# One block of the r, k and v groups' vectors on TensorE and three on VectorE, instead of two and two

## The reference

```python
def trunk(x, c, ...):
    cs = jax.nn.silu(c)                                   # one condition vector for prompt, one for sample
    for l in range(DEPTH):
        mod = (cs @ W['ada_w'][l] + W['ada_b'][l]).reshape(B, N_MOD, D)   # 6 vectors of 2048 each
        h = modulate(rmsnorm(x, W['norm_mix_g'][l]), mod[:, 0], mod[:, 1])
        ...
        r = (h + xx * mu[0]) @ p['wr']                    # 288 tokens x 2048 x 2048
        k = (h + xx * mu[2]) @ p['wk']
        v = xv @ p['wv']
```

## Time and profile before

| what | value |
|---|---|
| time, median of 3 runs | 3187.66 us (3185.27 to 3188.28) |
| profiled execution, its own time | 3181.33 us |
| its span | 3179.8 us |
| TensorE (PE) busy | 3099.7 us, 97% of the span |
| TensorE weight loads (PEld) busy | 2933.2 us, 92% |
| VectorE (DVE) busy | 2301.4 us, 72% |
| ScalarE (ACT) busy | 1405.9 us, 44% |
| stream loads | 1022 of 512 KB, 4.2 us from issue to landing (median) |

### The profile page before, as it was taken

The page is one execution under the profiler, slowest core; times in us unless marked ns, Lnnn a source line. Parts: engine busy times, 40 slices in busy tenths (PEclk is TensorE's granted clock), DMA queues, the critical chain, the costliest instruction groups (busy, mean ns, idle before and its releaser), DMA issues.

```text
span 3179.8 us, 80532 instructions
## 1 busy us (share of the span) xinstructions
PE 3099.7 (97%) x31192; PEld 2933.2 (92%) x31192; DVE 2301.4 (72%) x4445; ACT 1405.9 (44%) x2322; POOL 196.9 (6%) x371
## 2 busy tenths in 40 slices
PE   6999999998999999999999999999999999999998
PEld 3799988877999999999999989998999999999998
DVE  3676777776478978888788888778785566666655
ACT  2333336665355443343344744334455534343442
POOL 0000000110000000000000000101100000000000
PEclk8999999999999999999999999999999999999999
DMA  9887750003878887777777444644554455556443
GB/s 394 327 296 294 291 196 21 23 23 126 328 292 288 305 297 270 244 239 251 243 247 248 169 146 150 220 158 150 187 175 165 165 202 203 204 204 207 169 164 117
DMA packets 184093, 667.94 MB, mean 210 GB/s; under 512 B 22646, under 2 KB 22816, under 8 KB 183360
## 3 DMA queue, kind: packets, MB, share of 16 engines
q1 hardware_dynamic: 149184, 545.78, 47.3%
q0 software_dynamic: 34688, 119.07, 11.7%
HBM read 660.68 MB, written 4.09 MB: 209 GB/s over the span
## 4 chain that ended last, share of the span: by engine, by line
PE 91%; DMA 3%; DVE 3%; issue 1%; ACT 1%; SPq 0%; DVEq 0%; POOLq 0%; ACTq 0%
PE ps L2384 52%; PE ps L2367 8%; PE ps L2369 7%; PE ps L2368 7%; PE ps L2553 5%; DMA sb_raw<-stream 2%; PE ps L2318 1%; PE ps L2545 1%; DMA sb_late_w<-late 1%; PE ps L2883 1%; PE ps L2884 1%; PE ps L2885 1%; PE ps L2927 1%; PE ps L2926 1%; PE ps L2329 1%
## 5 line engine op out<-in xcount | busy, mean ns | idle before, releaser
L786 ACT ACTIVATE sb_whi<-sb_raw 128x1024 fp32r<-128x1024 f32 x778 | 811.0, 1057 | 1089.7 <-PE ps L2384 674.0
L1278 DVE TENSOR_TENSOR sb_wlo<-sb_raw,sb_whi 128x1024 fp32r<-128x1024 f32 x778 | 943.4, 1222 | 318.2 <-ACT sb_whi L786 315.5
L2384 PE MATMUL ps<-sb_ah,sb_whi 128*128 128x288 f32 (+1 forms) x2776 | 485.4, 297 | 1.2 <-DVE sb_wlo L1278 1.2
L2384 PE MATMUL ps<-sb_al,sb_whi 128*128 128x288 f32 (+1 forms) x2776 | 483.2, 296 | 0.0
L2384 PE MATMUL ps<-sb_ah,sb_wlo 128*128 128x288 f32 (+1 forms) x2776 | 481.1, 295 | 0.0
L2384 PEld LDWEIGHTS ps<-sb_ah,sb_whi 128*128 128x128 f32 x2776 | 408.6, 189 | 5.8 <-issue 3.1
L2384 PEld LDWEIGHTS ps<-sb_al,sb_whi 128*128 128x128 f32 x2776 | 408.0, 189 | 0.0
L2384 PEld LDWEIGHTS ps<-sb_ah,sb_wlo 128*128 128x128 f32 x2776 | 407.2, 188 | 0.0
L2367 PE MATMUL ps<-sb_ah,sb_whi 128*128 128x288 f32 (+1 forms) x952 | 286.5, 301 | 4.1 <-DVE sb_x L1531 3.2
L2369 PE MATMUL ps<-sb_al,sb_whi 128*128 128x288 f32 (+1 forms) x952 | 283.1, 297 | 0.0
L2368 PE MATMUL ps<-sb_ah,sb_wlo 128*128 128x288 f32 (+1 forms) x952 | 282.5, 297 | 0.0
(11 more groups left out here) (366 smaller groups left out, 4797.0 us busy)
## 6 DMA issues: line engine op xcount, KB each, us to landing
sb_raw<-stream SPq DMA_DIRECT2D x1022, 512.0 KB, 4.2
sb_strip<-strips POOLq DMA_DIRECT2D x124, 512.0 KB, 5.0
sb_late_w<-late POOLq DMA_DIRECT2D x96, 256.0 KB, 3.2
sb_gate_w<-late POOLq DMA_DIRECT2D x64, 256.0 KB, 3.6
sb_x<-xT SPq DMA_DIRECT2D x1, 2304.0 KB, 15.8
sb_x<-xT POOLq DMA_DIRECT2D x1, 2304.0 KB, 11.0
yT<-sb_x SPq DMA_DIRECT2D x4, 576.0 KB, 2.8
sb_lwa<-lw POOLq DMA_DIRECT2D x16, 130.0 KB, 2.5
```

The source lines that it names most:

```text
L786: nc.scalar.activation(whi[:, q % SPL, :], raw[:, n, :], ACT.Copy).then_inc(hi_ready, 1)
L1278: nc.vector.tensor_tensor(wlo[:, q % SPL, :], raw[:, n, :], whi[:, q % SPL, :], ALU.subtract).then_inc(lo_ready, 1)
L2384: ins = mm(PS[:, m, 0:s.wide], w[:, n % SPL, a:a + P], z[:, 2 * p + j, 0:s.wide], start=False, stop=False)
```

## The change

In the nine shared groups TensorE takes one block of vectors instead of two, and VectorE three instead of two. TensorE's block now fills two slots (`BURST_SLOTS`), buffers 0 and 1 of round A, and is done in 16 products of 2 x 128 columns. VectorE's three blocks fill six slots (`ROW_SLOTS`): buffers 2 and 3 of round A and 0 to 3 of round B. Row slot 0 and the copy to `arow` now stand behind the split of slot 2, row slot 1 behind that of slot 3, row slots 2 and 3 behind slot 4, row slot 4 behind slot 5 and row slot 5 behind slot 6. `half_finish` turns one block. The stream has as many bytes as before; SP's instructions are the same ones in the same order.

```diff
+ROW_SLOTS = 6
+BURST_SLOTS = 2 * BURST - ROW_SLOTS
+GROUP_ROWS = ROW_SLOTS // 2
+STAGE_BURSTS = 4 + 3
-SHARED_PLACES = ((), (0, 1), (2,), (3,), (), ())
+SHARED_PLACES = ((0,), (1,), (2, 3), (4,), (5,), ())
...
                 if shared(s, it):
-                    dve.wait_ge(ada_used, 2 * BURST * g + BURST)
+                    dve.wait_ge(ada_used, 2 * BURST * g + BURST_SLOTS)
...
-                if i == 2:
+                if i == 0:
                     row(s, it)
                 for j in SHARED_PLACES[i]:
                     one_row_strip(s, it, j)
...
-                dve.wait_ge(landed[j], it * s.span * 2 + 16 * ((s.n0 + RAW + j) // RAW + 1))
-                dve.wait_ge(ada_used, 2 * BURST * it + (2 * BURST * s.ada0 + BURST + j))
+                dve.wait_ge(landed[n % RAW], it * s.span * 2 + 16 * (n // RAW + 1))
+                dve.wait_ge(ada_used, 2 * BURST * it + (2 * BURST * s.ada0 + BURST_SLOTS + j))
                 for e in range(4):
                     a, z = e // 2, e % 2
...
-                        out=PS[:, 6 + z, :], in0=raw[:, j, ROW * a:ROW * a + ROW], scalar=1.0, in1=crows[z][:],
+                        out=PS[:, 6 + z, :], in0=raw[:, n % RAW, ROW * a:ROW * a + ROW], scalar=1.0, in1=crows[z][:],
...
                 pe.wait_ge(arow_ready, s.ada0 + it)
-                for p in range(BURST):
+                for p in range(BURST_SLOTS):
                     n = s.n0 + p
                     pe.wait_ge(landed[n % RAW], it * s.span * 2 + 16 * (n // RAW + 1))
-                    for z in range(4):
-                        ins = mm(PS[32 * z:32 * z + 2, 4, 0:256], cs[:, 4 * p + z, :], raw[:, n % RAW, 256 * z:256 * z + 256],
-                                 start=p == 0, stop=p == BURST - 1)
+                    for b in range(8):
+                        z = b % 4
+                        ins = mm(PS[32 * z:32 * z + 2, 4, 0:P], cs[:, 8 * p + b, :], raw[:, n % RAW, P * b:P * b + P],
+                                 start=p == 0 and b < 4, stop=p == BURST_SLOTS - 1 and b >= 4)
                     ins.then_inc(ada_used, 1)
...
-                for m in range(2):
+                for m in range(blocks):
                     ins = mm(PS[:, 5, 2 * m:2 * m + 2], arow[:, P * m:P * m + P], con[:, SEL + 4:SEL + 6],
                              start=True, stop=True)
...
                         if shared(s, it) and p == 6:
-                            half_finish(s.ada0 + it)
+                            half_finish(s.ada0 + it, 1)
```

More of the change, by code:

```diff
@@ L239 @@
 SHARED0 = BY["r"].ada0 * 4
-ROW_BLOCKS0 = SHARED0 + 10 * len(SHARED)
-SHARED_PLACES = ((), (0, 1), (2,), (3,), (), ())
+ROW_SLOTS = 6
+BURST_SLOTS = 2 * BURST - ROW_SLOTS
+GROUP_ROWS = ROW_SLOTS // 2
+STAGE_BURSTS = 4 + 3
+ROW_BLOCKS0 = SHARED0 + STAGE_BURSTS * len(SHARED)
+SHARED_PLACES = ((0,), (1,), (2, 3), (4,), (5,), ())
 ROW = HS // 2
-ROWS_USED = 3 * BURST * SHARED_GROUPS + 1
+ROWS_USED = 3 * ROW_SLOTS * SHARED_GROUPS + 1
 LATE_USED = ROWS_USED + 2 * STRIPS
@@ L344, in trunk @@
         crsig = sb("crsig", [P, 2, ROW], "K")
-        row_sums = sb("row_sums", [P, SHARED_GROUPS, 16], "MIDS", 4 * T * 4 + ROW * 4)
-        row_turned = sb("row_turned", [P, 4, 2 * SHARED_GROUPS, 2], "MIDS", 4 * T * 4 + ROW * 4 + SHARED_GROUPS * 64)
+        row_sums = sb("row_sums", [P, SHARED_GROUPS, 4 * ROW_SLOTS], "MIDS", 4 * T * 4 + ROW * 4)
+        row_turned = sb("row_turned", [P, 4, GROUP_ROWS * SHARED_GROUPS, 2], "WORK", 4 * TW * 4)
         parts = sb("parts", [P, STRIPS // 2, 4], "H", 2 * D * 4)
@@ L1312, in stage_mods @@
                     g = s.ada0 + it
-                    n = 2 if shared(s, it) else 4
-                    b = 2 * it + (SHARED0 + 10 * SHARED.index(s.name) + (2 if n == 2 else 0))
+                    n = 1 if shared(s, it) else 4
+                    b = it + (SHARED0 + STAGE_BURSTS * SHARED.index(s.name) + (3 if n == 1 else 0))
                     dve.wait_ge(ada_fin, g + 1)
@@ L1338, in one_row_strip @@
             def one_row_strip(s, it, j):
-                u = 3 * SHARED.index(s.name) - 1
+                u, n = 3 * SHARED.index(s.name) - 1, s.n0 + BURST_SLOTS + (j if BURST_SLOTS + j < BURST else j + BURST)
                 dve.wait_ge(silu_ready, 3)
-                dve.wait_ge(landed[j], it * s.span * 2 + 16 * ((s.n0 + RAW + j) // RAW + 1))
-                dve.wait_ge(ada_used, 2 * BURST * it + (2 * BURST * s.ada0 + BURST + j))
+                dve.wait_ge(landed[n % RAW], it * s.span * 2 + 16 * (n // RAW + 1))
+                dve.wait_ge(ada_used, 2 * BURST * it + (2 * BURST * s.ada0 + BURST_SLOTS + j))
                 for e in range(4):
@@ L1346, in one_row_strip @@
                     if e != 1:
-                        dve.wait_ge(strip_used, 3 * BURST * it + (3 * BURST * u + 3 * j + max(e - 1, 0) + 1))
+                        dve.wait_ge(strip_used, 3 * ROW_SLOTS * it + (3 * ROW_SLOTS * u + 3 * j + max(e - 1, 0) + 1))
                     ins = nc.vector.scalar_tensor_tensor(
-                        out=PS[:, 6 + z, :], in0=raw[:, j, ROW * a:ROW * a + ROW], scalar=1.0, in1=crows[z][:],
+                        out=PS[:, 6 + z, :], in0=raw[:, n % RAW, ROW * a:ROW * a + ROW], scalar=1.0, in1=crows[z][:],
                         op0=ALU.mult, op1=ALU.mult,
@@ L1357, in join_rows @@
                 dve.wait_ge(ada_used, 2 * BURST * BY["o"].ada0)
-                sums = row_sums[:].rearrange("p g (b q z) -> p (g b) q z", b=2, q=4)
+                sums = row_sums[:].rearrange("p g (b q z) -> p (g b) q z", b=GROUP_ROWS, q=4)
                 for c in range(4):
@@ L1363, in join_rows @@
                 b = ROW_BLOCKS0
-                out = mod[:, b:b + 2 * SHARED_GROUPS, :]
+                out = mod[:, b:b + GROUP_ROWS * SHARED_GROUPS, :]
                 ch.inc(nc.vector.tensor_tensor(out, row_turned[:, 0], row_turned[:, 1], ALU.add))
@@ L1369, in join_rows @@
                 ch.wait()
-                ch.inc(nc.vector.tensor_tensor(out, out, vec[:, ADAB + b:ADAB + b + 2 * SHARED_GROUPS].rearrange(
-                    "p (a t) -> p a t", t=1).to_broadcast([P, 2 * SHARED_GROUPS, 2]), ALU.add))
+                ch.inc(nc.vector.tensor_tensor(out, out, vec[:, ADAB + b:ADAB + b + GROUP_ROWS * SHARED_GROUPS].rearrange(
+                    "p (a t) -> p a t", t=1).to_broadcast([P, GROUP_ROWS * SHARED_GROUPS, 2]), ALU.add))
                 ch.wait()
@@ L2336, in shared_burst, with half_finish @@
                 pe.wait_ge(arow_ready, s.ada0 + it)
-                for p in range(BURST):
+                for p in range(BURST_SLOTS):
                     n = s.n0 + p
                     pe.wait_ge(landed[n % RAW], it * s.span * 2 + 16 * (n // RAW + 1))
-                    for z in range(4):
-                        ins = mm(PS[32 * z:32 * z + 2, 4, 0:256], cs[:, 4 * p + z, :], raw[:, n % RAW, 256 * z:256 * z + 256],
-                                 start=p == 0, stop=p == BURST - 1)
+                    for b in range(8):
+                        z = b % 4
+                        ins = mm(PS[32 * z:32 * z + 2, 4, 0:P], cs[:, 8 * p + b, :], raw[:, n % RAW, P * b:P * b + P],
+                                 start=p == 0 and b < 4, stop=p == BURST_SLOTS - 1 and b >= 4)
                     ins.then_inc(ada_used, 1)
-            def half_finish(g):
+            def half_finish(g, blocks=2):
                 pe.wait_ge(arow_ready, g + 1)
                 pe.wait_ge(mod_ready, g)
-                for m in range(2):
+                for m in range(blocks):
                     ins = mm(PS[:, 5, 2 * m:2 * m + 2], arow[:, P * m:P * m + P], con[:, SEL + 4:SEL + 6],
@@ L3061, in by_burst, with by_block @@
     return w.reshape(BURST, 4, P, m // 256, 256).transpose(3, 0, 2, 1, 4).reshape(-1, BURST, P, HS)
+def by_block(w):
+    kk, m = w.shape
+    return w.reshape(BURST_SLOTS, 8, P, m // P, P).transpose(3, 0, 2, 1, 4).reshape(-1, BURST_SLOTS, P, HS)
 def by_row(w):
     kk, m = w.shape
-    return w.T.reshape(m // 256, BURST, 2, 32, 4, kk // 4).transpose(0, 1, 4, 3, 2, 5).reshape(-1, BURST, P, HS)
+    return w.T.reshape(m // HC // 2, 2, HC, 4, kk // 4).transpose(0, 3, 2, 1, 4).reshape(-1, ROW_SLOTS, P, HS)
 def by_32(w):
@@ L3139 @@
     for i, n in enumerate(("rw_wr", "rw_wk", "rw_wv")):
-        at = P * (SHARED0 + 10 * i)
-        both = np.concatenate([by_burst(ada[0][:, at + 512:at + 1280]), in_rows[3 * i:3 * i + 3]], 1)
+        at = P * (SHARED0 + STAGE_BURSTS * i)
+        both = np.concatenate([by_block(ada[0][:, at + 512:at + P * STAGE_BURSTS]), in_rows[3 * i:3 * i + 3]], 1)
         parts.append(woven(np.concatenate([vectors(ada[0][:, at:at + 512]), both.reshape(-1, P, HS)], 0), halves(a[n][0])))
```

## The result

The changed kernel takes 3279.5 us (median of 4 runs, 3276.11 to 3280.57) against 3187.26 us for the kernel before beside it: a ratio of 1.0292, 95% interval 1.028 to 1.0305. It is slower by 92 us; 3273 us were predicted, in a range of 3254 to 3298. The profiled execution took 3278.8 us, its span 3277.3 us.

A forecast was written before the change was run, and what follows sets the result against it. TensorE was taken to set the pace before, two round trips a shared group after. Losses of 28.7, 28.7 and 28.0 us in r, k and v, 85.4 us, added to 3187.7 gave 3273 us, range 3254 to 3298.

The forecast's parts named there:

- Which wait comes late, and where: In shared groups, VectorE waits a round trip before slot 4's split and another before the next group's slot 0.
- Its length: Wait from VectorE's row slot through SP, DMA and ScalarE to VectorE's next split, taken as 6.5 us.
- the trips: Waits from a row slot's end to the next split in r, k and v: 17 on the path, 6.5 us each.
- The turn: From one shared group's last row slot to the next one's: 18.4 plus 20.5 us, 38.9 us together.
- the tiles' 1.3 us: In stage v, tiles that VectorE sets up on the path were counted as 1.3 us.
- the stretch from the split of slot 0 to that of slot 2: Part of each shared group's first half, set by landings and ScalarE, taken as 4.15 us.
- The sum: Time lost over r, k and v: 28.7 + 28.7 + 28.0 = 85.4 us.
- What was left out: Stages behind v were expected to stay as they were; joining more columns of row sums was too little to count.
- VectorE's cost: Two more row slots per shared group raise VectorE's work from 20.28 to about 25.5 us, still under 28.
- TensorE's gain: Shorter bursts save 0 to 1.09 us in each of nine groups, counted as nothing; rival that it arrives, chance 0.02.
- The clock: Waits before slot 4 may lower TensorE's clock, 10.2 us hidden; rival that it stays low, 3413 us, chance 0.06.

The follow-up runs named there:

- e7_one_trip: The changed kernel with SP loading buffers in order 0, 1, 4, 5, 6, 7, 2, 3 only in each group's second round; ratio 1.0107 to the kernel before.
- e1_order: The changed kernel with SP loading each round's buffers in order 0, 1, 4, 5, 6, 7, 2, 3 in r, k and v; 3198.12 us.
- e4_no_idle: The changed kernel with 18 idle 128 x 128 products on TensorE before slot 4 of each shared group; ratio 1.028 to the kernel before.
- e8_even: The changed kernel, load order 0, 1, 4, 5, 6, 2, 3, 7, ScalarE's bank 0 copy later, one row slot behind each split of slots 2-7; 3179.81 us.
- e6_short_burst: The kernel before with the 16 products of each shared burst on 128 columns instead of 256; ratio 0.9985 to the kernel before.

## Why the prediction was right

**Which wait comes late, and where.** Shown: the load of slot 4 behind row slot 1, the load of the next slot 0 behind row slot 5, by the timelines, by SP's waits, and by taking away one (e7_one_trip) and both (e1_order).

**Its length.** 6.5 us were taken from the kernel before. In k's group 2 the trips were 343.73 - 337.25 = 6.5 and 364.11 - 357.75 = 6.4 us. All 17 of the trace lie between 6.28 and 7.24 us, 6.55 on average; fewer transfers in flight did not shorten them.

**The turn.** 38.9 us predicted. From one group's last row slot to the next one's, as the prediction counts, 38.1 to 38.9 were measured in five turns, and 39.8 in v's last, which holds the tiles' 1.3 us (40.2 predicted). Bursts stood 36.7 us apart once (r's group 2) and otherwise 38.1 to 38.9, where the prediction asked for 38 to 40. The term that was a little off is the stretch from the split of slot 0 to that of slot 2: 4.15 us taken from one place, 3.64 us there now (325.88 to 329.52).

**The sum.** 85.4 us predicted for r, k and v, 85.5 measured. Slot 0 of k began at 260.70 against 261.7. That the tenths agree is luck: r lost 27.7 us, k 28.4 and v 29.4, where 28.7, 28.7 and 28.0 were predicted. The turn was half a microsecond too long, and v's last group lost 1.2 us more than was counted behind its last row slot.

**What was left out.** Behind v I counted nothing, and the profiled executions differ there by 12 us. 8.9 us of it are in the lanes, which vary as much without any change; another 2.3 us lie near the start of the last MLP, where the granted clock dipped once. The medians of the timed runs differ by 92.2 us, 6.7 more than the lanes' start, and that carries the result from 3273 to 3279.5. That the change causes it is not shown, and one run speaks against it: e4_no_idle has all of the change, and its profile took 2718.8 us from the start of the lanes to the end, the kernel before 2719.1, the changed kernel 2731.1. Why it varies stays open.

**VectorE's cost** was right as a sum (25.5 us predicted, 25.39 measured) and right not to be the point. **TensorE's gain** was right to count as nothing. Its ceiling was close too: 1.09 us a group, 1.07 where all waits were out of the way (e8_even).

**The clock** went the way of the prediction: mean 0.87 to 0.95 in the shared groups, no time lost behind slot 4. The Trainium skill (TensorE: Matmul & The Clock Gate, HAM oscillation — how this bites in real kernels) says that a loop with such a wait in every turn can fall to the lower clock each time and pay for it each time. The trace agrees on the falls. That each of them costs does not hold for slot 4 here (e4_no_idle, 3.6 us later and not earlier), where something slower than the array sets the turn.

## What to carry to other kernels

When work moves from one engine to another, ask which buffers it now holds and what stands behind their reload in the queue; an in-order queue makes a transfer wait for the slowest consumer in front of it, and an engine's sum of work says nothing of that. Here 73.7 of 85.5 us hung on the order of the eight loads in a round. And a gain on the busiest engine is worth only the distance to the next limit: 0.86 us a group were taken off TensorE in e6_short_burst, and between bursts 0.31 to 0.85 us came out. In the changed kernel 1.07 us came out, once the loads, the copy and the row slots stood in another order (e8_even).

## What the runs showed of the hardware

- The same lane loop took 285 to 298 us from run to run, with no edit in it (288 to 298 us in four runs on one chip). What varies there stays open; single profiles of this kernel should not be compared by their total to better than some 10 us.
- 32 matmul records of 2 x 128 columns took 0.98 us and those of 2 x 256 columns 1.84 us, so the time of these two-row products fell nearly with their columns.
- Turning the burst's result took 0.36 us for two blocks and 0.14 us for one where TensorE did not wait (e8_even).
- TensorE's mean granted clock fell to 0.91 over a group with one wait of 4.75 us and shorter ones; with that wait filled by idle products it was 0.91 to 0.96 in k's three groups, and there it fell after a wait of 3.17 us as well (e4_no_idle: the four products behind that wait took 1.07 us instead of 0.79).
